# One copy of the head weights, modulation items in four pairs, and eight expert places in a one-core transformer block

## The chip, the cores and the metric

The kernel runs on one core of a Trainium2 chip. The metric is the device time of one execution in microseconds (us), the median of several. A profile of one execution gives its span, from the first to the last instruction, and a trace of every instruction. PE is TensorE, DVE is VectorE, ACT is ScalarE, POOL is GpSimd, SP is SyncE, whose queue issues nearly all loads here.

## The reference

One layer on 256 tokens of width 1024, all in float32:

```python
mod = c_act @ w_ada + b_ada                      # 6 x 1024: shift, scale, gate for both halves
h = rms_norm(x) * (1 + scale1) + shift1
z = h @ w_in                                     # 3 conv inputs, q/kv latents, rope key, 2 gates
merged = sigmoid(zg_conv) * conv_branch + sigmoid(zg_mla) * attention_branch   # 8 heads of 128
x = x + gate1 * (merged @ w_o)
h2 = rms_norm(x) * (1 + scale2) + shift2
x = x + gate2 * moe(h2)                          # 4 groups x 8 experts, top 1 group, top 2 experts
```

Each of the 32 experts has a gate-up matrix (1024 x 512) and a down matrix (256 x 1024).

## The kernel before, in words

Each engine has one instruction stream, written out by hand with semaphores between them. The work goes through five stages.

**Prologue.** Four of the twelve modulation items (`ada_half`, 2 MiB each) and the latent projections run on PE as their weights land.

**Eight heads.** PE's loop over `h` does for each head: the q and k projections, attention output of the head before (`attend`), tile 0 of the next head's five input projections (`conv_tile(h + 1, 0, ...)`, each 8 contraction steps), the v projection (`v_ready`), sums of squares, tiles 1 (`zxc_ready`) and 2, then a wait on `kq_ready` and the scores (`s_ready`), the column sums of one modulation item, tile 3 (`zbg_ready`), tile 4 (`zgm_ready`), and the transposes of the probabilities. In the last head `project_early` puts parts of the output projection in the place of the next head's tiles. A multiplication of 128x128 by 128x256 in float32 is recorded as two instructions.

The other eight modulation items are summed on DVE: `ada_steps` multiplies eight slices of 512 columns with a column of the conditioning vector and adds them up. Steps 0 to 4 stand behind `conv_gated` of the head before; steps 5 to 7 (L1042, L1044) stand ahead of the rotary part of q (L1064, L1065), the reciprocal (L1069) and the normalised keys (L1070, L1071), the last of which gives `kq_ready`. Then come the convolution taps (L1012 to L1016) and the reductions of the scores (L1086, L1088).

The weights of a head (3 MiB: five tiles of 0.5 MiB and the small q, kv matrices) go in one piece into one of the two halves of `wmix`, while the other half is in use. A modulation item goes in one piece (2 MiB) into the region of expert place 3. SP's loop over `c` issues: item `c + 1` after `ada_summed`, weights of head `c + 2` after `v_ready`, and for `c` 1 to 3 expert `c - 1` whole (3 MiB).

**Transition.** The output projection ends; DVE adds it to x (L1120); ACT squares; PE forms the router's logits and sums of squares (`lgt_ready`); DVE copies them (L1126); PE folds them; ACT and DVE do the routing; `select` (L1180 to L1184) gives the first one-hot selection (`sel_ready`). In the meantime PE turns x into rows (`turn_x2`) and opens the four output banks: `open_with_residual` starts tiles 2, 3, 6, 7 with x, `open_empty` starts two banks with nothing.

**Experts.** Tokens of each expert are gathered in windows of 32. A window does on PE: the gate-up product (64 instructions of 128x128), the next window's `gather`, a transpose, `combine` of the window before, `turn_rows`, the down product. Every expert has at least one window; here 35 windows run, and the trace shows experts 2, 3 and 28 with two each. Expert `e` lies in place `e % 7`: four places in `wex`, two in `wmix`, and one split over `act2` and `work`. SP's `next_expert` loads expert `e + 7` into the place of expert `e` as soon as its windows are through: gate-up after `gu_ready`, down after `down_ready`, or both in one piece after `down_ready` in the middle of the list. Half of expert 28's down matrix is loaded ahead into free tiles of `xT`. The loop runs 4 times over 7 places and 4 more experts are written out behind it.

**End.** Two output banks are added to x by DVE and stored by SP; two are copied by ACT (L528) and stored by ACT's queue.

Of the kernel before, what the change touches and what calls it, by code (L numbers as in the profile page):

```python
# [6 lines left out]
I32 = mybir.dt.int32  # L7
# [6 lines left out]
P = 128  # L14
# [48 lines left out]
WO_COLS = KT * 4 * P  # L63
GU_COLS = 2 * KT * FF
DOWN_COLS = (FF // P) * D
EX_SLOTS = 7
OWN = 4
WINDOWS = EXPERTS + SLOTS // WIN
GATE_HEAD = HEADS - 2
FIRST_TILES = 2 * KT * P  # L70
TAIL = EXPERTS - EXPERTS % EX_SLOTS
WORK = 6824
# [3 lines left out]
def block_kernel(nc, xT_d, pos_d, small_d, const_d, ada_d, lat_d, mix_even_d, mix_odd_d, wo_d, ex_d, out_d):  # L76
    with ExitStack() as ctx:
# [8 lines left out]

        wex = sb("wex", [P, OWN, GU_COLS + DOWN_COLS])
        wmix = sb("wmix", [P, GU_COLS + DOWN_COLS + MIX_COLS[0]])
        ring_slot = [wmix[:, 0:GU_COLS + DOWN_COLS], wmix[:, GU_COLS + DOWN_COLS:]]

        ex_place = [wex[:, s, :] for s in range(OWN)] + [ring_slot[1 - s][:, 0:GU_COLS + DOWN_COLS] for s in range(2)]
# [11 lines left out]
        c_rep = sb("c_rep", [P, KT, WIN])  # L103
# [15 lines left out]

        q_lat = piece(3 * T).rearrange("p (k n) -> p k n", k=3)  # L120
# [4 lines left out]
        q_x = piece(T)  # L125
# [5 lines left out]
        v_sb = piece(2 * P).rearrange("p (a b) -> p a b", a=2)  # L131
        rms = piece(2 * T)
        rk_s, rk = rms[:, 0:T], rms[:, T:2 * T]
        scores = piece(P + T)
        probs = piece(P + T)
        pT = piece(P + T)
        zx = piece(T)
        t_gate = piece(T)
        m_gate = piece(T)
        conv_t = piece(T)  # L140
        o_t = zx
        u = piece(T + 2)
        stat = piece(16)
        posi, posf = q_x.bitcast(I32), k_r
# [17 lines left out]
        e_work = piece(2 * 64).rearrange("p (a t n) -> p a t n", a=2, t=TT)  # L162
        s_work = piece(24).rearrange("p (a t) -> p a t", a=12)
        oh = piece(3 * 64).rearrange("p (a t n) -> p a t n", a=3, t=TT)
        slots = piece(64).rearrange("p (t n) -> p t n", t=TT)
        slot_oh = piece(128).rearrange("p (c t n) -> p c t n", c=2, t=TT)
        slot_tok = piece(4).rearrange("p (c t) -> p c t", c=2)
        turn_by = hT[:, 0:KT // 2, :].rearrange("p a n -> p (a n)").rearrange("p (k c) -> p k c", k=KT)
        x2_sq = [hT[:, 4:6, :], hT[:, 6:8, :], comb_both.rearrange("p (k n) -> p k n", k=2), work[:, TT * WIN + 4 * WIN:TT * WIN + 4 * WIN + 2 * T].rearrange("p (k n) -> p k n", k=2)]
        logits_t, sq_sums = hT[:, 4, :], hT[:, 5, :]  # L170
        rs_tok, r_tok = s_work[:, 10, :], s_work[:, 11, :]
        split_tail = piece(GU_COLS // 2 + DOWN_COLS)

        split_head = act2[:, 0:KT, :].rearrange("p a n -> p (a n)")

# [1173 lines left out]
```

## Time and profile before

| | |
|---|---|
| time, median of 3 runs | 501.27 us (500.9 to 501.34) |
| span of the profiled execution | 499.3 us |
| time of the profiled execution by itself | not given; the median run is 2.0 us above the span |
| PE busy | 481.4 us, 96% of the span |
| DVE, ACT, POOL busy | 241.3, 136.6, 152.8 us |
| read from HBM | 160.5 MB, 324 GB/s over the span |
| mean granted clock of PE | 0.992 |

PE is the engine that nearly always works, so a change shows where it alters a wait of PE. The slices of the DMA line say in which stages transfers run without a pause. Of 1 MiB transfers the bytes are 1,048,576.

### The profile page before, as it was taken

Reading aid. Unit: us, or ns where it says so; the run is one execution under the profiler, and the core shown is the slowest. Engines: PE = TensorE matmul, PEld = TensorE weight load, DVE = VectorE, ACT = ScalarE, POOL = GpSimd, SP = SyncE. Lnnn points to the kernel's source line nnn. Section 1 sums busy time; section 2 is a strip of 40 time slices with the busy share of each in tenths; the row PEclk is TensorE's granted clock in tenths of the full one; section 3 lists DMA queues with packets and bytes.
Section 4 is the critical chain, followed back from the end, with each engine's and each line's share of the span. In section 5 each row is a group of like instructions: output and inputs, shape, how many; then the busy total and the mean of one; then the engine's idle time right before and its main releaser. Section 6 shows DMA issues by size and latency. Waiting matters only on the chain.

```text
span 499.3 us, 14059 instructions
## 1 busy us (share of the span) xinstructions
PE 481.4 (96%) x5769; PEld 378.1 (76%) x5770; DVE 241.3 (48%) x647; ACT 136.6 (27%) x243; POOL 152.8 (31%) x195
## 2 busy tenths in 40 slices
PE   8899999999999999999999999999999999888895
PEld 6678888888888888888888877767767766556563
DVE  1433765656565656456651455344344344332343
ACT  4013122323222232313232362232232232221231
POOL 0000010101010101010100018777777777665673
PEclk9999999999999999999999999999999999998998
DMA  8999318295969590907073999899999999999992
GB/s 324 423 424 425 164 53 379 58 433 202 427 258 425 219 407 25 408 8 296 42 291 130 362 411 430 358 394 422 434 437 427 421 441 427 421 423 428 424 403 95
DMA packets 13711, 162.02 MB, mean 324 GB/s; under 512 B 1648, under 2 KB 1904, under 8 KB 3568
## 3 DMA queue, kind: packets, MB, share of 16 engines
q1 hardware_dynamic: 13392, 161.04, 78.1%
q8 instruction: 24, 0.39, 0.3%
q10 hardware_dynamic: 288, 0.52, 0.3%
q14 instruction: 7, 0.06, 0.0%
HBM read 160.51 MB, written 1.05 MB: 324 GB/s over the span
## 4 chain that ended last, share of the span: by engine, by line
PE 83%; DMA 14%; DVE 2%; ACT 0%; issue 0%; ACTq 0%; DVEq 0%
PE ps L536 79%; DMA wex<-in_ex 14%; PE ps L839 1%; PE ps L879 1%; PE ps L840 1%; DVE work L958 0%; ACT xT L528 0%; PE ps L755 0%; PE ps L753 0%; PE ps L754 0%; DVE act L973 0%; DVE act L961 0%; PE ps L739 0%; ACT work L431 0%; DVE work L1223 0%
## 5 line engine op out<-in xcount | busy, mean ns | idle before, releaser
L536 PE MATMUL ps<-act,wmix 128*128 128x256 f32 x864 | 195.0, 381 | 1.7 <-DVE act L973 1.7
L536 PEld LDWEIGHTS ps<-act,wmix 128*128 128x128 f32 x864 | 161.1, 190 | 25.9 <-issue 4.6
L412 POOL TENSOR_SCALAR work<-trig,work 128x256 f32<-128x256 f32 x70 | 64.9, 937 | 57.3 <-issue 48.1
L398 POOL TENSOR_TENSOR work<-work,trig 64x256 f32<-64x256 f32 x8 | 5.8, 719 | 237.0 <-ACT work L466 141.6
L536 PE MATMUL ps<-work 32*128 32x256 f32 (+6 forms) x864 | 72.8, 374 | 0.6 <-DVE work L1223 0.6
L536 PE MATMUL ps<-wex,work 128*32 128x128 f32 (+1 forms) x1824 | 65.6, 295 | 3.7 <-DMA wex<-in_ex 3.7
L536 PEld LDWEIGHTS ps<-wex,work 128*32 128x32 f32 x1824 | 49.8, 110 | 16.8 <-issue 8.4
L536 PEld LDWEIGHTS ps<-work 32*128 32x128 f32 (+3 forms) x864 | 47.6, 168 | 13.3 <-issue 3.3
L524 ACT ACTIVATE work<-ps 128x64 f32<-128x64 f32 x35 | 7.8, 224 | 139.9 <-PE ps L879 139.9
L524 ACT ACT_TABLE_LOAD x35 | 44.9, 1283 | 1.8 <-issue 0.3
L416 POOL TENSOR_TENSOR work<-work,trig 128x512 f32<-128x512 f32 x35 | 44.5, 1271 | 0.0
L536 PE MATMUL ps<-act,work 128*32 128x256 f32 (+1 forms) x704 | 42.9, 362 | 0.9 <-DVE work L1183 0.6
L419 POOL TENSOR_TENSOR work<-work 128x256 f32<-128x256 f32 x35 | 25.5, 727 | 37.3 <-PE ps L536 37.2
L1042 DVE SCALAR_TENSOR_TENSOR wex<-wex,c_rep 128x512 f32<-128x512 f32 x48 | 36.0, 751 | 1.6
L536 PE MATMUL ps<-wmix,work 128*32 128x128 f32 (+2 forms) x704 | 33.3, 304 | 3.3 <-DMA wmix<-in_ex 3.3
L1208 DVE COPY work<-ps 128x128 f32<-128x128 f32 x35 | 10.2, 292 | 54.2 <-PE ps L536 54.2
L536 PEld LDWEIGHTS ps<-wmix,work 128*32 128x32 f32 (+1 forms) x704 | 27.0, 121 | 8.4 <-issue 5.6
L1216 DVE TENSOR_TENSOR work<-ps,mod 128x256 f32<-128x256 f32 x35 | 14.9, 425 | 33.9 <-PE ps L840 33.9
L536 PEld LDWEIGHTS ps<-act,work 128*32 128x32 f32 x704 | 22.4, 111 | 8.3 <-DVE work L1216 0.7
L1211 DVE COPY work<-ps 128x256 f32<-128x256 f32 x35 | 14.9, 425 | 20.6 <-PE ps L536 20.6
L536 PE MATMUL ps<-work,wmix 128*128 128x256 f32 x104 | 23.8, 379 | 0.0
L536 PEld LDWEIGHTS ps<-work,wmix 128*128 128x128 f32 x104 | 19.2, 190 | 2.3
(200 smaller groups left out, 432.2 us busy)
## 6 DMA issues: line engine op xcount, KB each, us to landing
wex<-in_ex SPq DMA_DIRECT2D x10, 3072.0 KB, 22.4
wex<-in_ex SPq DMA_DIRECT2D x10, 2048.0 KB, 24.1
wex<-in_ada SPq DMA_DIRECT2D x8, 2048.0 KB, 7.7
wmix<-in_ex SPq DMA_DIRECT2D x4, 3072.0 KB, 20.9
wmix<-in_mix_odd SPq DMA_DIRECT2D x4, 3008.0 KB, 15.5
wmix<-in_mix_even SPq DMA_DIRECT2D x3, 3200.0 KB, 16.1
wex<-in_ex SPq DMA_DIRECT2D x9, 1024.0 KB, 11.4
wex<-in_ada SPq DMA_DIRECT2D x8, 1024.0 KB, 16.7
```

Source lines behind the costliest of these rows:

```text
L398: nc.gpsimd.tensor_tensor(k_sq[0:ROPE, :], k_sq[0:ROPE, :], k_rope_sq[0:ROPE, :], ALU.add).then_inc(sq_joined, 1)
L412: nc.gpsimd.tensor_scalar(comb_both[:, rows], slot_row[:, rows], lane_now, None, ALU.is_equal).then_inc(comb_half, 1)
L416: nc.gpsimd.tensor_tensor(comb_both, comb_both, weight_row, ALU.mult).then_inc(comb_pair, 1)
L419: nc.gpsimd.tensor_tensor(comb, comb_both[:, 0:T], comb_both[:, T:2 * T], ALU.add).then_inc(comb_ready, 1)
L524: nc.scalar.activation(silu_t, ps[:, 1, 0:2 * WIN], ACT.Silu).then_inc(silu_done, 1)
L536: return nc.tensor.matmul(out, lhsT, rhs, start=start, stop=stop, **kw)
L839: nc.tensor.transpose(ps[:, 0, P:2 * P], rows_sb[:, 0:P], ident)
L840: nc.tensor.transpose(ps[:, 0, 2 * P:3 * P], rows_sb[:, P:T], ident).then_inc(rows_turned, 1)
L1042: link(v.scalar_tensor_tensor(ada_sum, w[:, k, :], c_rep[:, k, 0:1], ada_sum, ALU.mult, ALU.add))
L1208: v.tensor_copy(gu_sb, ps[:, 0, 0:P]).then_inc(gu_copied, 1)
L1211: v.tensor_copy(rows_sb, ps[:, 3, 0:T]).then_inc(rows_copied, 1)
L1216: v.tensor_tensor(xw_v, xw_ps, shift2, ALU.add).then_inc(xw_ready, 1)
```

## The change

- The weights of a head are held once: `conv_w` (five tiles) and `small_w`. SP loads the next head's tiles 0 and 1, tiles 2 and 3, tile 4 and the small matrices as four transfers, each as soon as PE has read the present head's (`zxc_ready`, `zbg_ready`, `zgm_ready`, `v_ready`).
- A modulation item is loaded as four pairs of slices of 0.5 MiB, through two slots (`ada_pair`). `ada_pair_step(j, i)` on DVE waits for pair `i` and does two slices. Pairs 0 and 1 stand where steps 0 to 4 stood, pair 2 where steps 5 to 7 stood, pair 3 behind `kq_ready`, ahead of the taps.
- One region `wex` holds the head weights, the pairs and six expert places in turn; there are eight expert places. Ahead of the loop over `c`, SP issues half the gate-up of expert 5 and all of expert 4; expert `c - 1` for `c` 1 to 4 comes in two pieces; the down matrix of expert 7 goes into `xT` after `residual_in`, and all eight tiles of x are opened into the output banks.
- The output weights come in five transfers into the freed head weights and pairs.
- The memset of `ycomb` and two small copies stand behind `lgt_ready`.
- Experts run in 4 rounds of 8 with nothing behind them. The results are copied to `out_tiles` in place of an addition.

```diff
-EX_SLOTS = 7
+EX_SLOTS = 8
...
+            tiles_load(0, 0, 2, tiles01_landed)
...
+            small_w_load(0)
             sp.dma_start(small[:, SMALL_FIRST:], small_d[:, SMALL_FIRST:]).then_inc(router_landed, 16)
+            pair_load(0, 0)
+            pair_load(0, 1)
+            sp.wait_ge(zxc_ready, 1)
+            tiles_load(1, 0, 2, tiles01_landed)
+            sp.wait_ge(zbg_ready, 1)
+            tiles_load(1, 2, 2, tiles23_landed)
+            sp.wait_ge(zgm_ready, 1)
+            tiles_load(1, 4, 1, tile4_landed)
+            gu_half_load(OWN + 1, OWN + 1, 0)
+            whole_load(OWN, OWN)
             for c in range(HEADS):
+                sp.wait_ge(pair_summed, 4 * c + 1)
+                pair_load(c, 2)
+                sp.wait_ge(pair_summed, 4 * c + 2)
+                pair_load(c, 3)
+                if 1 <= c <= OWN:
+                    gu_load(c - 1, c - 1)
+                sp.wait_ge(v_ready, c + 1)
                 if c + 1 < HEADS:
-                    beside_load(c + 1)
-                if c + 2 < HEADS:
-                    mix_load(c + 2)
...
+                    small_w_load(c + 1)
+                    sp.wait_ge(pair_summed, 4 * c + 3)
+                    pair_load(c + 1, 0)
+                    sp.wait_ge(zxc_ready, c + 2)
...
+                    sp.wait_ge(pair_summed, 4 * c + 4)
+                    pair_load(c + 1, 1)
+                    if 1 <= c <= OWN:
+                        down_load(c - 1, c - 1)
...
+            wo_load(7, 1, wo_w[7], wo7_landed)
+            sp.wait_ge(pair_summed, 4 * HEADS)
+            wo_load(5, 2, wex[:, ADA_AT:ADA_AT + 2 * ADA_PAIR], wo56_landed)
+            head_load(SPLIT, SPLIT)
+            sp.wait_ge(s_ready, HEADS)
+            tail_load(SPLIT, SPLIT)
+            sp.wait_ge(wo_ready, 1)
+            gu_half_load(OWN + 1, OWN + 1, 1)
+            sp.wait_ge(wo_ready, 2)
+            down_load(OWN + 1, OWN + 1)
+            sp.wait_ge(wo_ready, 4)
+            gu_load(LAST, LAST)
             sp.wait_ge(residual_in, 1)
+            down_load(LAST, LAST)
...
-            open_with_residual(7).then_inc(residual_in, 1)
+            open_with_residual(7)
             pe.wait_ge(lg_done, 1)
-            open_empty(2)
+            open_with_residual(4)
+            open_with_residual(5)
             pe.wait_ge(h2r_copied, 4)
-            open_empty(0)
+            open_with_residual(0)
+            open_with_residual(1).then_inc(residual_in, 1)
...
+            def ada_pair_step(j, i):
+                w = ada_pair[i % 2].rearrange("p (k c) -> p k c", k=2)
+                dve.wait_ge(pair_landed[i % 2], 32 * j + 16 * (i // 2) + 16)
+                if i == 0:
+                    dve.wait_ge(c_ready, 2)
                     dve.wait_ge(ada_done, 4 + j)
+                    link(v.tensor_scalar(ada_sum, w[:, 0, :], c_col[:, 0:1], None, ALU.mult))
+                else:
+                    link(v.scalar_tensor_tensor(ada_sum, w[:, 0, :], c_col[:, 2 * i:2 * i + 1], ada_sum, ALU.mult, ALU.add))
+                v.scalar_tensor_tensor(ada_sum, w[:, 1, :], c_col[:, 2 * i + 1:2 * i + 2], ada_sum, ALU.mult, ALU.add).then_inc(pair_summed, 1)
...
                     link(v.tensor_tensor(q_r, q_x, cos_t, ALU.mult))
-                    ada_steps(h, range(5, KT))
+                    ada_pair_step(h, 2)
                     dve.wait_ge(swap_ready, h // 2 + 1)
...
                 v.tensor_tensor(k_r[rope, :], k_rot[rope, :], rk[rope, :], ALU.mult).then_inc(kq_ready, 1)
+                ada_pair_step(h, 3)
                 if h + 1 < HEADS:
                     conv_taps(h + 1)
...
+            dve.wait_ge(lgt_ready, 1)
+            v.memset(ycomb, 0.0).then_inc(y_copied, 1)
             v.tensor_copy(slot_now, co("slot_no"))
             link(v.tensor_copy(lane_now, co("lane_no")))
-            dve.wait_ge(lgt_ready, 1)
             v.tensor_copy(logits_t, ps[:, 5, 0:T]).then_inc(lgt_copied, 1)
```

## Rows read from the trace of the kernel before

**Rows 1.** The page: busy tenths of PE and of the DMA engines in 40 slices

```profile
PE   8899999999999999999999999999999999888895
DMA  8999318295969590907073999899999999999992
```

**Rows 2.** Busy time in stretches: PE, PEld, DVE, ACT, POOL, then clock, DMA share, GB/s

```profile
110.00:135.00 25.00, 25.00 (x131) 21.34 (x130) 15.05 (x32) 7.55 (x17) 1.40 (x2) 1.00 0.76 310
```

**Rows 3.** Timeline of PE among the experts: start, length, line, tiles, [idle before, releaser]

```profile
430.73 1.95 PE L536 MATMUL ps<-wex,work 128*32 128x128 f32 x64 [1.79 <-DMA wex<-in_ex]
...
450.38 3.29 PE L536 MATMUL ps<-wmix,work 128*32 128x128 f32 x64 [1.85 <-DMA wmix<-in_ex]
...
457.83 1.08 PE L536 MATMUL ps<-act,work 128*32 128x128 f32 x32 [0.26 <-DMA work<-in_ex]
...
465.27 1.95 PE L536 MATMUL ps<-wex,work 128*32 128x128 f32 x64 [1.91 <-DMA wex<-in_ex]
...
485.91 2.82 PE L536 MATMUL ps<-wex,work 128*32 128x256 f32 x80
```

**Rows 4.** Timeline of PE, from head 0's tiles to its scores

```profile
49.63 13.98 PE L536 MATMUL ps<-act,wmix 128*128 128x256 f32 x64
63.44 3.62 PE L536 MATMUL ps<-work,wmix 128*128 128x256 f32 x16
...
72.55 7.07 PE L536 MATMUL ps<-act,wmix 128*128 128x256 f32 x32
79.46 2.05 PE L536 MATMUL ps<-work 128*128 128x128 f32 x8
```

**Rows 5.** Transfers: alone at 323.9 (2 MiB), then KB and us to landing

```profile
L283 SPq DMA_DIRECT2D wex<-in_ex x1: 331/331/331, 323.9 to 323.9; - x1
DMA to landing us min/median/max: 7.5/7.5/7.5
...
wex<-in_ada SPq DMA_DIRECT2D x8, 2048.0 KB, 7.7
...
xT<-in_xT SPq DMA_DIRECT2D x1, 1024.0 KB, 5.0
```

**Rows 6.** Timeline of DVE in head 0

```profile
69.28 1.54 DVE L1042 SCALAR_TENSOR_TENSOR wex<-wex,c_rep 128x512 f32<-128x512 f32 x2
...
72.75 0.42 DVE L1064 TENSOR_TENSOR work<-trig,ps 128x256 f32<-128x256 f32 x1 [1.15 <-PE ps L536]
...
75.94 0.42 DVE L1071 TENSOR_TENSOR work<-trig,work 64x256 f32<-64x256 f32 x1
...
81.55 0.29 DVE L1086 CUSTOM_DVE_ANT_0 work<-ps,const 128x128 f32<-128x128 f32 x1 [2.89 <-PE ps L536]
```

**Rows 7.** Clock and PE's busy time in one stretch

```profile
450.80:454.00 3.20, 3.20 (x65) 0.50 1.01 417
```

**Rows 8.** DVE in head 1; DVE and PE in head 7

```profile
98.80 1.75 DVE L1069 RECIPROCAL work<-work 128x256 f32<-128x256 f32 x1 [2.42 <-ACT work L476]
...
256.32 0.42 DVE L1071 TENSOR_TENSOR work<-trig,work 64x256 f32<-64x256 f32 x1
...
261.82 7.17 PE L536 MATMUL ps<-act,wmix 128*128 128x256 f32 x32
```

**Rows 9.** DVE, then PE, in the transition

```profile
274.46 0.48 DVE L1114 MEMSET work<- 128x512 f32 x1
...
281.17 0.17 DVE L1122 COPY work<-const 128x32 f32<-128x32 f32 x1
...
283.35 0.42 DVE L1126 COPY act<-ps 128x256 f32<-128x256 f32 x1 [1.96 <-PE ps L536]
...
289.27 1.54 PE L536 MATMUL ps<-xT,const 128*128 128x256 f32 x6
290.65 0.50 PE L536 MATMUL ps<-work,const 128*128 128x1 f32 x4
291.79 1.07 PE L536 MATMUL ps<-act,work 128*32 128x256 f32 x16 [0.64 <-DVE work L1183]
```

More of the change, by code:

```diff
@@ L118, in piece @@
             return work[0:parts, a:a + cols]
+        v_sb = piece(2 * P).rearrange("p (a b) -> p a b", a=2)
+        scores = probs = piece(P + T)
+        pT = piece(P + T)
+        zx = piece(T)
+        m_gate = piece(T)
+        stat = piece(16)
+        conv_t = piece(T)
+        o_t = zx
+        u = piece(T + 2)
+        c_rep = work[:, 256:256 + KT * WIN].rearrange("p (k n) -> p k n", k=KT)
+        assert work_at[0] <= WORK - 2 * CHUNK_COLS
+        work_at[0] = WORK - 2 * CHUNK_COLS
         q_lat = piece(3 * T).rearrange("p (k n) -> p k n", k=3)
@@ L187, in block_kernel @@
[L187 to L191 removed]
+            if place == SPLIT:
+                half, at = (split_head, split_tail)[k // (KT // 2)], k % (KT // 2)
+                return half[:, 2 * FF * at:2 * FF * (at + 1)]
+            return (ex_place[place] if place < SPLIT else last_gu)[:, 2 * FF * k:2 * FF * (k + 1)]
@@ L358, in _, with tiles_load @@
-            down_load(OWN - 1, OWN - 1)
-            last = EX_SLOTS - 1
-            sp.wait_ge(merged_ready, HEADS)
-            tail_load(last, last)
-            for n in range(2):
-                sp.wait_ge(wo_ready, 2 * n + 2)
-                whole_load(OWN + n, OWN + n)
-            sp.wait_ge(h2r_ready, 2)
-            sp.wait_ge(lg_ready, 1)
-            head_load(last, last)
+            def tiles_load(h, first, count, landed):
+                at = slice(first * CONV_TILE, (first + count) * CONV_TILE)
+                sp.dma_start(conv_w[:, at], (mix_even_d, mix_odd_d)[h % 2][h // 2][:, at]).then_inc(landed, 16)
@@ L552, in ada_half @@
                     pe.wait_ge(ada_copied, n - 1)
-                last = ada_item(wex[:, n, 0:ADA_COLS], ps[:, (0, 5)[n % 2], 0:P], range(half * KT // 2, (half + 1) * KT // 2))
+                last = ada_item(ex_place[n][:, 0:ADA_COLS], ps[:, (0, 5)[n % 2], 0:P], range(half * KT // 2, (half + 1) * KT // 2))
                 if half == 1:
@@ L905, in _ @@
                     next_bound()
-            for e in range(ROUNDS * EX_SLOTS, EXPERTS):
-                with passes() as n:
-                    window(e % EX_SLOTS, ROUNDS + 1, n, e + 2 if e + 2 <= EXPERTS else None, e == TAIL)
-                next_bound()
             at = pe.snap(bound_at, min_val=1, max_val=WINDOWS)
@@ L1109, in _ @@
                     conv_gated(h + 1)
-                    ada_steps(h + 1, range(0, 5))
+                    for i in range(2):
+                        ada_pair_step(h + 1, i)
             merge(HEADS - 1)
-            v.memset(ycomb, 0.0).then_inc(y_copied, 1)
             v.memset(wins[:, 0:1], 0.0)
+            v.memset(table[0:1, EXPERTS + 1:EXPERTS + 2], 0)
             dve.wait_ge(mod_ready, HEADS)
@@ L1323 @@
     ada = np.stack([kcols(w) for w in first] + [kcols(wa[:, n * 512:(n + 1) * 512]) for n in range(4, ADA_ITEMS)])
-    wo = np.stack([tiles(a["w_o"][0][:, n * 512:(n + 1) * 512], 4) for n in range(2)])
+    wo = tiles(a["w_o"][0], 8)
     gate = a["w_exp_gate"][0].reshape(EXPERTS, KT, P, FF)
```

262 lines of the change are left out of this document (128 added, 134 removed).

## The prediction

> **What bounds the kernel now.** I read the slices of the page first [rows 1]: PE is busy nearly throughout, while the transfers pause again and again among the heads and never among the experts. The stretches then say that PE has no idle time at all in a head [rows 2], with the DMA engines at 0.76. So among the heads PE sets the time, and a transfer or a DVE step costs nothing until it makes PE wait. Last I read PE's timeline among the experts [rows 3]. PE waits there for gate-up weights: 1.79, 1.85, 0.26 and 1.91 us in these rows, and once more for 1.44 us in a like row between the first two, 7.25 us in all. The 64 instructions behind the 1.85 us wait take 3.29 us in place of 1.95, and the 16 behind them 1.46 in place of 1.05, at a granted clock of 0.50 [rows 7]: 1.75 us more. So the transfer stream costs about 9.0 us there. Successive landings of experts lie 7.44 us apart (450.38, 457.83, 465.27) for 3 MiB, so 2.48 us per MiB.
>
> **Eight places, among the experts.** The load released at 323.9 by the second window of expert 3 lands 7.5 us later, like a 2 MiB load alone (7.7) [rows 5]. So the queue had run dry there; from then on it never pauses. Before, this load is expert 10. After, with eight places, it is expert 11, and all earlier ones are through, since expert 10 was released 10.6 us sooner (two windows of 5.3 us) and needs 7.4. The stream is then one expert ahead: expert 28's gate-up lands when expert 27's did, at 457.8 and not 465.3. Expert 28's down matrix now comes whole, so from there to expert 31's gate-up are 9 MiB: 457.8 + 22.3 = 480.1. PE began expert 31's gate-up at 485.91 + 1.0 = 486.9 [rows 3] (that row starts with the 16 down instructions). Four windows lie between it and expert 28's first, 486.9 - 465.3 = 21.6 us; after, PE would come to it at 457.9 + 21.6 = 479.5, so the transfer decides at 480.2. Gain 6.7 us. Bounds: at 1% more bandwidth the stream gives 8; 5.7 if the clock falls at expert 28's wait, which I put at 1.6 us (465.3 - 9.0 = 456.3 for PE against 457.9): 1.75 us lost less 0.7 us of slack. I take 6.7.
>
> **Head 0: expert weights ahead of a pair.** SP issues in order. At the end of tile 4, about 63.6 [rows 4], it issues tile 4 of head 1 (0.5 MiB), half of expert 5's gate-up (1 MiB), expert 4 (3 MiB), and only then pair 2 of item 0 (0.5 MiB). The queue is empty before, as tiles 2 and 3 left 3.5 us earlier. A load alone takes 5.0 us for 1 MiB and 7.5 for 2 [rows 5]: 2.5 plus 2.5 per MiB. The pair lands at 63.6 + 2.5 + 5 x 2.48 = 78.5. DVE wants it at 69.28 [rows 6], and DVE is in order: the rotary part, the reciprocal and the keys stand behind it. From the landing: two slices 1.55 us (the row of two is 1.54), then 3.6 us as from 72.75 to the end of 75.94, so `kq_ready` at 83.7. PE wants it at 79.46, when tiles 1 and 2 are through [rows 4]. PE waits 4.2 us. Behind it pair 3 (1.5) and the taps (1.9) delay the score reductions to 87.2; scores end at 85.7, and the transposes come 9.4 us behind the start of the scores, so nothing more is late. Bounds: 0 if the order of the queue did not hold; 5.5 at 2.6 us per MiB and 0.5 us more of start. I take 4.2.
>
> [...]
>
> **The clock behind that wait.** The only fall of the clock with work waiting came behind a 1.85 us wait; waits of 1.79 and 1.91 us drew none [rows 3, 7]. A wait of 4.2 us is twice as long as any of them, so I take a fall, at the price seen: 1.7 us. Bounds: 0 and, if the low level lasts twice as long, 3.4.
>
> **The other heads.** Tiles 2 and 3, tile 4 and pair 2 (2 MiB) are issued from 3.9 us ahead of a head's start to its start, so pair 2 lands some 4 to 5 us into the head. DVE takes it up 5.8 us in (63.44 to 69.28), about 1 us sooner in an odd head. If it is late, the reciprocal still has 2.4 us of waiting ahead of it [rows 8] and one slice fewer (0.77). Cost nothing; cover about 3 us. A head loads at most 8.1 MiB, 20.1 us of its 25.5. Pair 3 puts 1.5 us ahead of the taps, inside the 2.89 us that DVE waits for the scores [rows 6]. Tiles of the next head have 15 us each to land. In head 7 the output weights of tiles 5 and 6 are issued at 256.7 + 1.6 = 258.3 and land at 263.3; PE wants them six steps into 261.82, at 264.4 [rows 8]. Nothing, with 1.1 us of cover; a microsecond late would cost nothing, two would cost one.
>
> **The transition.** The memset is 0.43 to 0.48 us [rows 9], the two copies 0.2 to 0.25, and they now stand between `lgt_ready` and the copy at 283.35, whose end PE waits for: +0.65. Four openings with x replace two empty ones. An opening is 1.54/3, less overlap 0.43. The three ahead end at 290.6; four more end at 292.3, past the 291.79 at which the selection is ready [rows 9]: +0.5. Bounds 0.8 and 1.5 for both. The windows themselves, the four rounds and the copies at the end change nothing that PE or the last store waits for.
>
> **Sum.** -6.7 + 4.2 + 1.7 + 0.65 + 0.5 = +0.35 us on the 499.3 us span. The median of the runs stands 2.0 us above the span; I keep that: 501.27 + 0.35 = 501.6. A difference under 0.2% (1.0 us) is what this measurement can't tell from none.
>
> **Rivals.**
> - *The pair is not late* (0.14). SP's order stands against it; for it only that no 4.5 MiB lie ahead of a small load in this trace among the heads. Then the 4.2 and the 1.7 fall away: -5.5, 495.7 us.
> - *The clock holds* (0.14). The waits of 1.79 and 1.91 us speak for it, their shortness against. -1.35: 499.9 us.
> - *The clock is low for longer, and again at expert 28* (0.12). +0.35 + 1.7 + 1.0: 504.3 us.
> - *Small transfers are too slow* (0.10): every head waits for pair 2. It decides once pair 2 is more than 3 us later than I reckon. Each 0.5 us beyond costs 3.5 us over seven heads, so 505 us and more. Against it: 1 MiB alone lands in 5.0 us [rows 5], on the line of the 2 MiB loads. [...]
> - My forecast has 0.50.
>
> **Chances.** Within the forecast my error is some 1.2 us either way: of its 0.50, 0.06 is faster by over 0.2%, 0.26 within, 0.18 slower. The case of the holding clock splits 0.09 faster, 0.05 within. With the others: faster 0.29, same 0.31, slower 0.40. The likeliest case alone spans 500.0 to 503.5. The range of all reaches down towards the pair in time and up over the longer fall: 497.0 to 504.5.
>
> **What would show it.** In PE's timeline a wait of about 4 us ahead of head 0's scores, released by DVE, with DVE waiting about 9 us for a transfer ahead of its sixth slice; a granted clock of 0.50 behind it. The first window then starts some 7 us later than before. Among the experts waits of at most 3 us in all, at expert 28 and 31 only. If PE does not wait in head 0, the kernel is faster. If waits for pairs or tiles come in every head, or the waits among the experts stay above 5 us, it is slower.

## The result, and the profile after

The changed kernel takes 545.58 us (median of 4 runs, 543.71 to 547.58) beside 501.3 us for the kernel before on the same chip: ratio 1.0879, interval 1.0841 to 1.0916. That is 44 us slower, where 501.6 us was forecast. The profiled execution has a span of 542.0 us against 499.3, so 42.7 us are to be found in it.

The page of the kernel after, the slices and the queues that answer to [rows 1]:

```profile
PE   8899998999999999999999799985998599859995
...
PEclk9999997999999999999999899997999799979998
DMA  8993694989798987455457299999899999999102
...
q1 hardware_dynamic: 21456, 161.04, 75.2%
q8 instruction: 49, 0.80, 0.6%
```

PE's row now has deep notches among the experts, at even distances, where [rows 1] shows 8 and 9, and the clock dips behind each. The bytes of q1 are what the kernel before moved. The queue of instructions, q8, moved 0.80 MB in 49 transfers; on the page of the kernel before that line reads `q8 instruction: 24, 0.39, 0.3%`. One transfer is 16.3 KB. The trace of the kernel before has 13 of these transfers ahead of the experts, 7 in the first round of its loop (290 to 345 us), none in the three rounds from 345 to 469 us, and 4 behind the loop. After, there are 13, then 8 up to 365 us, and 28 more in the rounds behind.

Head 0, the timelines of DVE and of PE (what answers to [rows 4, 6]):

```profile
78.80 0.75 DVE L1092 SCALAR_TENSOR_TENSOR wex<-wex,c_col 128x512 f32<-128x512 f32 x1 [9.19 <-DMA wex<-in_ada]
...
83.53 0.42 DVE L1123 TENSOR_TENSOR work<-trig,work 64x256 f32<-64x256 f32 x1
```

```profile
84.00 3.06 PE L587 MATMUL ps<-work 128*128 128x128 f32 x8 [3.94 <-DVE work L1123]
```

Pair 2 of item 0 is usable at 78.80, where 78.5 was reckoned, and PE waits 3.94 us for the keys. The scores start at 84.00 instead of 79.46; 0.4 of these 4.5 us come from the prologue, 4.1 from the pair.

The clock behind that wait, and the stretches of PE among the experts (busy PE, PEld, DVE, ACT, POOL, then clock, DMA share, GB/s):

```profile
84.00:92.00 8.00, 8.00 (x27) 5.25 (x28) 4.69 (x15) 1.32 (x5) 0.00 (x0) 0.57 0.41 152
335.00:380.00 45.00, 37.11 (x713) 25.70 (x717) 14.71 (x51) 10.55 (x14) 25.18 (x32) 0.92 0.93 383
...
507.00:533.00 26.00, 26.00 (x571) 18.48 (x571) 11.58 (x40) 6.85 (x10) 20.18 (x25) 1.00 0.01 3
```

And PE's timeline among the experts, where [rows 3] had waits for weights:

```profile
308.31 3.64 PE L587 MATMUL ps<-wex,work 128*32 128x128 f32 x64 [3.93 <-issue]
...
362.61 0.51 PE L587 MATMUL ps<-wex,work 128*32 128x128 f32 x9 [2.07 <-issue]
...
372.62 3.64 PE L587 MATMUL ps<-wex,work 128*32 128x128 f32 x64 [5.82 <-issue]
376.03 1.94 PE L587 MATMUL ps<-act,work 128*32 128x256 f32 x16
...
392.39 1.36 PE L587 MATMUL ps<-wex,work 128*32 128x128 f32 x41 [0.19 <-issue]
...
398.47 1.14 PE L587 MATMUL ps<-wex,work 128*32 128x128 f32 x33 [0.16 <-issue]
...
405.12 0.93 PE L587 MATMUL ps<-wex,work 128*32 128x128 f32 x25 [0.74 <-issue]
...
411.54 0.71 PE L587 MATMUL ps<-work 128*32 128x128 f32 x17 [0.51 <-issue]
...
418.97 0.52 PE L587 MATMUL ps<-wex,work 128*32 128x128 f32 x9 [1.52 <-issue]
...
429.36 3.64 PE L587 MATMUL ps<-wex,work 128*32 128x128 f32 x64 [6.20 <-issue]
...
484.83 3.37 PE L587 MATMUL ps<-wex,work 128*32 128x128 f32 x64 [5.96 <-issue]
```

The waits of PE from 270 us on (us in total, times, longest):

```profile
PE ps L587 <- issue: 29.8, 15, 6.2
```

**Where the 42.7 us are.** The first gate-up starts at 308.31 instead of 294.99, 13.3 us later: 8.0 from the heads (the transposes of head 0's probabilities already come 7.9 later, and it stays so), 1.3 from the transition, 4.0 from the wait at the loop's entry. From there to the last down projection the kernel after takes 227.3 us, the one before 197.9: 29.4 more. That is 25.9 us of waits on issue (29.8 less the one at the entry), plus the low clock behind four long ones. Behind the wait at 372.62, 64 matmuls take 3.64 instead of 1.95 us and the next 16 take 1.94 instead of 1.05: 2.6 us. The same stands behind 308.31 and 429.36; behind 484.83 it is 1.4, as the 16 already take 1.04 there: 9.2 for the four. 25.9 + 9.2 less the 9.0 us that the stream cost before is 26.1 of the 29.4. The rest goes with the short waits: the window with the wait of 1.52 us at 418.97 takes 7.24 us instead of 5.31, so 0.4 us more than the wait explains, and there are eleven of them.

### The profile page after: what moved, and what is told of

The parts are those of the page before. It is cut to its first block, busy times and chain, and to the rows that moved or that the text cites. A ratio compares the mean times of both kernels' runs of the same rounds, so it can differ in the third digit from the quotient of the medians.

```text
span 542.0 us, 14151 instructions
## 1 busy us (share of the span) xinstructions
PE 497.5 (92%) x5773; PEld 387.7 (72%) x5774; DVE 238.8 (44%) x648; ACT 136.7 (25%) x244; POOL 152.4 (28%) x195
## 3 DMA queue, kind: packets, MB, share of 16 engines
HBM read 160.51 MB, written 1.05 MB: 298 GB/s over the span
## 4 chain that ended last, share of the span: by engine, by line
PE 82%; DMA 7%; issue 6%; SPq 2%; DVE 2%; ACT 0%; ACTq 0%; DVEq 0%
PE ps L587 77%; DMA wex<-in_ada 7%; PE ps L935 2%; PE ps L896 2%; PE ps L897 1%; SPq L292 1%; SPq L328 0%; DVE work L1121 0%; SPq L339 0%; ACT wex L579 0%; PE ps L813 0%; PE ps L815 0%; PE ps L814 0%; DVE wex L1093 0%; DVE wex L1092 0%
## 5 line engine op out<-in xcount | busy, mean ns | idle before, releaser
L587 PE MATMUL ps<-act,wex 128*128 128x256 f32 x864 | 197.1, 384 | 1.6 <-DVE act L1024 1.6
L587 PEld LDWEIGHTS ps<-act,wex 128*128 128x128 f32 x864 | 162.7, 192 | 26.6 <-issue 4.9
L587 PE MATMUL ps<-wex,work 128*32 128x128 f32 (+2 forms) x2736 | 112.6, 304 | 29.5 <-issue 29.0
L587 PEld LDWEIGHTS ps<-wex,work 128*32 128x32 f32 (+1 forms) x2736 | 87.8, 117 | 51.7 <-issue 40.1
L587 PE MATMUL ps<-act,work 128*32 128x256 f32 (+1 forms) x704 | 46.4, 372 | 0.0
L587 PEld LDWEIGHTS ps<-act,work 128*32 128x32 f32 x704 | 25.5, 114 | 7.3 <-issue 1.4
L1093 DVE SCALAR_TENSOR_TENSOR wex<-wex,c_col 128x512 f32<-128x512 f32 x32 | 24.1, 752 | 1.1
L1266 DVE COPY work<-ps 128x256 f32<-128x256 f32 x35 | 14.9, 425 | 21.9 <-PE ps L587 21.9
L587 PE MATMUL ps<-work,wex 128*128 128x256 f32 x104 | 23.9, 379 | 0.0
L1092 DVE SCALAR_TENSOR_TENSOR wex<-wex,c_col 128x512 f32<-128x512 f32 x24 | 18.0, 749 | 11.1 <-DMA wex<-in_ada 10.6
L587 PEld LDWEIGHTS ps<-work,wex 128*128 128x128 f32 x104 | 19.2, 190 | 2.5
L1121 DVE RECIPROCAL work<-work 128x256 f32<-128x256 f32 x8 | 14.0, 1754 | 11.9 <-ACT work L527 11.7
```

The costliest lines, as they stand in the source:

```text
L587: return nc.tensor.matmul(out, lhsT, rhs, start=start, stop=stop, **kw)
L1092: link(v.scalar_tensor_tensor(ada_sum, w[:, 0, :], c_col[:, 2 * i:2 * i + 1], ada_sum, ALU.mult, ALU.add))
L1093: v.scalar_tensor_tensor(ada_sum, w[:, 1, :], c_col[:, 2 * i + 1:2 * i + 2], ada_sum, ALU.mult, ALU.add).then_inc(pair_summed, 1)
L1121: link(v.reciprocal(rk, rk_s))
L1266: v.tensor_copy(rows_sb, ps[:, 3, 0:T]).then_inc(rows_copied, 1)
```

## The experiments

Each time is a median beside the kernel before in the same comparison (501.1 to 501.8 us). "Waits" are PE's waits among the experts.

### Is it the code? Written out, padded, and two other suspects

`a_unroll`: the kernel after, its four rounds written out as 32 windows.

```
-            with nc.Fori(0, ROUNDS, engines=[pe.engine], head_slot={pe.engine: 0}) as i:
-                for s in range(EX_SLOTS):
+            for e in range(EXPERTS):
```

> The changed kernel with its 32 experts written out on PE, in place of a loop of 4 rounds over 8 places; nothing else differs. Theory A (code loading): a loop body of 8 windows (8 x 230 recorded PE instructions) doesn't stay in PE's instruction memory, is loaded anew in each round, and PE waits for it. Written out, every instruction is loaded once and in order, as the last four windows of the kernel before were: the waits put down to issue fall from 29.8 us to under 5, and the time to 504 to 508 us. Theory B (the eight places or the smaller descriptor scratch slow the experts by themselves): the time stays above 535 us. Theory C (each jump back costs, not the size): as A in time, but the instruction queue would still carry some 0.8 MB; under A it carries about the same 0.8 MB too, so this run does not tell A from C; the padded loop does.

Measured: 532.92 us, ratio 1.0613 (1.0591 to 1.0635). Better than the loop, but far from the 504 to 508 expected. The wait at the entry is gone, and the others are shorter and still there: 17.3 and 3.2 us, with 0.70 MB on q8. So the jump back is only a part of it. Code in a straight line also comes late, while the stream of weights runs.

`b_pad60`: the kernel before with 60 matmuls at the end of the loop body that are never run; only the body is longer.

```
+                with pe.If(pe.snap(bound_at, min_val=0, max_val=WINDOWS) < 1):
+                    for _ in range(60):
+                        mm(ps[:, 0, 0:P], ident, ident, True, True)
```

> The kernel before (loop over 7 places) with 60 matmuls, some 240 instructions or one window's worth, written into the loop body behind a branch that is never taken; they never run. The next bound is also taken as the larger of 1 and the loaded value. Theory A (size of the body): the body is now as long as that of 8 windows, so the three rounds load it anew: instruction traffic rises from 0.39 MB to 0.6 to 0.8 MB, PE waits for issue some 15 to 30 us, and the time is 515 to 540 us. Theory B and C (places, scratch, jumps): nothing of these is changed, so 501 us within 1 us.

Measured: 544.27 us, ratio 1.0841 (1.0819 to 1.0863), above the 515 to 540 expected. All of the loss, in the old kernel, by code that does nothing. PE's timeline and the queue:

```profile
354.20 3.64 PE L536 MATMUL ps<-wex,work 128*32 128x128 f32 x64 [10.94 <-issue]
...
373.21 1.36 PE L536 MATMUL ps<-wex,work 128*32 128x128 f32 x41 [0.33 <-issue]
...
408.90 3.64 PE L536 MATMUL ps<-wex,work 128*32 128x128 f32 x64 [11.37 <-issue]
```

```profile
q8 instruction: 52, 0.85, 0.7%
```

The same pattern as after: a long wait once a round (10.9 to 11.4 us here and 10.8 to 11.4 in `b_pad32` below, in place of 5.8 to 6.2 after), then short ones, 41.6 us in all. Both jump over their unused part too; that this makes the long wait longer is my guess, no run tests it by itself.

`b_scratch`: the kernel before with the kernel after's `dynamic_dma_scratch_size=1024` and its form of the loop bound (all kernels here that start from the one before have that form).

> The kernel before with the descriptor scratch of the changed kernel (1024) and the bound taken as the larger of 1 and the loaded value. Theory A: no change, 501.3 within 1 us. Theory B (scratch or the register operation slows the experts): some of the 44 us appear, above 510 us.

Measured: 501.12 us, ratio 0.9988 (0.9973 to 1.0003). No effect. Ruled out.

`a_unroll_order`: written out, and the expert loads behind the pairs in head 0.

```
-            gu_half_load(OWN + 1, OWN + 1, 0)
-            whole_load(OWN, OWN)
             for c in range(HEADS):
...
                 pair_load(c, 3)
+                if c == 0:
+                    gu_half_load(OWN + 1, OWN + 1, 0)
+                    whole_load(OWN, OWN)
```

> As a_unroll, and the loads of half of expert 5 and of expert 4 stand behind pairs 2 and 3 of item 0 in SP's order. The queue theory of the prediction: head 0's wait ahead of the scores (4 us) and the low clock behind it go, 6 to 8 us less than a_unroll. Rival (the pair is late for another reason, or the low clock has another cause): within 2 us of a_unroll.

Measured: 524.64 us, ratio 1.0431 (1.0396 to 1.0467): 8.3 us less than `a_unroll`. That is the price of the order in SP's queue with the clock behind it; in the trace of after it is 4.1 us of wait and 3.3 of low clock. The waits on issue stay (18.8 us), now at the pace of the code:

```profile
408.48 1.83 PE L588 MATMUL ps<-wex,work 128*32 128x128 f32 x58 [0.48 <-issue]
415.05 1.61 PE L588 MATMUL ps<-wex,work 128*32 128x128 f32 x50 [0.64 <-issue]
421.34 1.39 PE L588 MATMUL ps<-wex,work 128*32 128x128 f32 x42 [0.36 <-issue]
427.49 1.17 PE L588 MATMUL ps<-wex,work 128*32 128x128 f32 x34 [0.22 <-issue]
```

Behind these waits PE goes on at points 6.2 to 6.6 us apart, while PE runs through 256 instructions in 5.7 by my estimate (5.31 us a window of 240).

### Why is the code late, and how long may the body be?

`a_unroll_light`: as `a_unroll_order`, but each load of experts 8 to 31 brings only a quarter of its bytes. It leaves that out of the computation: those experts run partly on old weights.

```
-                    whole_load(s, e + EX_SLOTS)
+                sp.dma_start(part, ex_d[e + EX_SLOTS][:, 0:GU_COLS // 4]).then_inc(gu_landed[s], 16)
...
+                sp.dma_start(place_down(s)[:, 0:DOWN_COLS // 4], ex_d[e + EX_SLOTS][:, GU_COLS:GU_COLS + DOWN_COLS // 4]).then_inc(down_landed[s], 16)
```

> As a_unroll_order, but each load of experts 8 to 31 brings only a quarter of its gate-up and of its down matrix (0.75 MiB in place of 3), so from expert 8 on the products use partly old weights; PE's program is the same. Theory D (instruction blocks are late because they share the DMA engines with a stream that never pauses): the waits for issue in the straight code, 19.5 us in a_unroll_order, fall under 3 us, and the time from 524.6 to 500 to 506. Rival E (the straight code is too long for PE whatever the queues do: blocks load at a fixed pace): the waits and the 524 us stay.

Measured: 491.33 us, ratio 0.979 (0.9769 to 0.9811), below the 500 to 506 expected. Its stretch from 380 to 430 us, and that of `a_unroll_order` below:

```profile
380.00:430.00 50.00, 50.00 (x1086) 35.22 (x1086) 22.45 (x77) 14.29 (x19) 37.93 (x47) 1.00 0.52 152
```

```profile
380.00:430.00 50.00, 46.09 (x908) 32.11 (x912) 18.31 (x63) 10.62 (x15) 32.38 (x40) 0.97 1.00 424
```

The same code, the same 0.70 MB on q8, and not one wait on issue once the DMA engines are busy at 0.52 instead of 1.00. So in this straight code the blocks are late because of the stream of weights. A block's own transfer takes some 1.0 us beside the full stream and 1.1 beside the light one (43 transfers in 0.5% and 0.6% of 16 engines' span), so it is not slower beside the stream; what is late is its start, and whether it queues at the DMA engines or waits for something else these runs don't separate. The run also shows the floor: 35 windows back to back end at 491.3 us.

`a_cut_order` and `b_cut`: gate-up over 6 of its 8 steps, on the kernel after (with the loads behind the pairs) and on the kernel before. Both leave a quarter of gate-up out. By the same count a window then has 208 instructions, eight of them 1,664.

```
-                for k in range(KT):
+                for k in range(6):
```

> The changed kernel with its loop of 4 rounds over 8 places, expert loads behind the pairs as in a_unroll_order, and the gate-up product over 6 of its 8 contraction steps (the other two are left out), so a window has 32 PE instructions less. The body is then shorter (8 x 213 by my count) than that of seven full windows (7 x 245). Theory A (size): no waits for issue, instruction traffic near 0.4 MB as before, and since the transfers now set the end, it is 4 to 6 us faster than b_cut: one expert ahead less the half down matrix, plus the transition. Rival (eight places cost by themselves): waits for issue stay, or it is no faster than b_cut.

> The kernel before with the gate-up product over 6 of its 8 contraction steps; the control of a_cut_order. PE has 0.44 us less per window, but the transfer stream sets the end: 496 to 499 us, with more waits for gate-up weights than the 7 us of before. If PE set the end it would be 486.

Measured: 501.02 us, ratio 0.9976 (0.9959 to 0.9994), and 498.56 us, ratio 0.9933 (0.9911 to 0.9955). In the first q8 fell to 0.34 MB and the waits on issue to 6.5 us, 4.1 of them at the entry. The size of the body is thus borne out, the time is not: `a_cut_order` was to end 4 to 6 us ahead of `b_cut` and ends 2.5 behind, as its wait at the entry was not foreseen. The gain among the experts can still be read: the one on eight places starts its first gate-up 5.5 us later (300.50 against 294.99) and its profiled span ends 1.1 later (499.9 against 498.8), so 4.4 us were made up (3.0 by the medians, since the profiled `b_cut` is its slowest run), in spite of 2.4 us of waits on issue behind the entry. It waits 11.8 us for weights, the one on seven places 17.1.

`b_pad24` and `b_pad32`: the kernel before with 24 and with 32 never-run matmuls in the body.

> The kernel before with 24 matmuls (96 instructions) behind a branch that is never taken, in the loop body; the bound as in b_pad60. By my count the body is then some 1810 instructions, against 1715 of before and 1960 of b_pad60. Theory A says only that there is a limit between the first and the last. If the limit is seven blocks of 256 (1792), some 30 to 43 us are lost here too; if it is nearer to eight, the time is 501 us. [...]

> The kernel before with 32 never-run matmuls in the loop body, about 1,816 of PE's instructions a round against 1,784 with 24 of them and some 1,926 with 60. If only seven blocks of 256 instructions (1,792) stay beside the running one, blocks are fetched again: q8 moves well over 0.39 MB and the time is over 515 us. If eight blocks (2,048) stay, nothing is fetched again: 0.39 MB and 501 to 503 us.

Measured: 502.18 us, ratio 1.0011 (0.9998 to 1.0025), and 543.49 us, ratio 1.0856 (1.0823 to 1.089). The rows of the queue, of 24 and of 32:

```profile
q8 instruction: 24, 0.39, 0.3%
```

```profile
q8 instruction: 51, 0.84, 0.7%
```

Eight matmuls that are never run, 32 instructions, cost 41 us. With 24 of them nothing is fetched again, and the waits on issue are 1.3 us in all. By my count the bodies have 1,784 and 1,816 instructions (seven windows of 240 are some 1,686 with what the loop itself needs, and a matmul is 4: two records on PE and two weight loads). The end of seven blocks of 256, at 1,792, lies between them. The 1,810 of `b_pad24`'s expectation came from 245 instructions a window; the shift by 16 in 256 says 240. The edge itself is shown only to within these eight matmuls. Eight windows of 240 are 1,920.

### The order alone, and the loop's entry alone

`a_order`: the kernel after in its own loop, with only the order of loads of `a_unroll_order`. It moves the loads of experts 5 and 4; the expectation misnames them.

> The kernel after, in its own loop of eight places, with the loads of expert 7's first half and of expert 6 moved behind pairs 2 and 3 of item 0. Theory: the wait of head 0 goes with the low clock behind it, worth 8.3 us in the written-out kernels, and the fetch stalls among the experts stay as long as they were (some 30 us): 536 to 539 us. Rival: the fetch stalls change with the earlier start by several us either way, since they depend on where blocks are asked for while the stream runs: outside 533 to 542.

Measured: 537.99 us, ratio 1.0715 (1.0667 to 1.0763), 7.6 us less than after, with 32.8 us of waits on issue beside 29.8. The scores of head 0 come without a wait:

```profile
79.70 2.06 PE L588 MATMUL ps<-work 128*128 128x128 f32 x8
```

> The kernel after with one thing changed: the loop's head is not set to the start of a block. The 3.9 us wait at the entry goes, as it did in the folded form (5.8 us with the clock behind it); the fetching again each round stays (q8 0.8 MB, over 20 us of waits on issue): 538 to 542 us. If the place of the head also changes how late the blocks come, it is outside that.

Measured: 538.69 us (537.17 to 544.12), ratio 1.0775 (1.0725 to 1.0825), 6.9 us less than after by the medians and 5.2 by the ratios. The wait at the entry is gone, q8 and the other waits (26.8 us) are not:

```profile
304.37 1.96 PE L587 MATMUL ps<-wex,work 128*32 128x128 f32 x64
...
383.73 1.40 PE L587 MATMUL ps<-wex,work 128*32 128x128 f32 x43 [0.20 <-issue]
...
390.00 1.18 PE L587 MATMUL ps<-wex,work 128*32 128x128 f32 x35 [0.34 <-issue]
```

The interrupted groups have 43 and 35 matmuls left instead of 41 and 33, so the body lies only a few instructions elsewhere. By that reading the setting may add a jump in front of the loop, over the filling up to the block's start; no trace shows the jump itself. The stream is not the cause of this wait: in the trace of after the DMA engines are at 0.24 during it, and one block comes on q8. All kernels here that start from the one after and have the setting wait 3.8 to 4.1 us at the entry; those that start from the one before have the same setting and no such wait. Why, was not found.

### Eight places in a body that fits

A window is so long because gate-up is 32 matmuls of four instructions each (64 records and 64 weight loads in the trace). Fewer, wider matmuls into the four quadrants of PSUM, each holding a part of the sum over k, need fewer; what turns the result then also adds the parts. All of this section's kernels do the whole computation. Those on the kernel after also have the loads behind the pairs and the copy of the logits ahead of the fill and the slot copies.

`a_fold`, `b_fold`: gate-up as 8 matmuls of 512 columns, four turning matmuls in place of the transpose; on eight and on seven places.

```
-                for k in range(KT):
-                    for q in range(4):
-                        last = mm(ps[q * WIN:(q + 1) * WIN, 0, 0:P], xw[:, k, :], place_gu(place, k)[:, q * P:(q + 1) * P], k == 0, k == KT - 1)
+                for k in range(KT):
+                    j = k % 4
+                    last = mm(ps[j * WIN:(j + 1) * WIN, 0, :], xw[:, k, :], place_gu(place, k), k < 4, k >= 4)
...
-                nc.tensor.transpose(ps[:, 1, 0:P], gu_sb, ident).then_inc(gu_turned, 1)
+                for q in range(4):
+                    last = mm(ps[:, 1, q * WIN:(q + 1) * WIN], gu_sb[:, q * P:(q + 1) * P], fold_by, True, True)
+                last.then_inc(gu_turned, 1)
```

> The kernel after with the loads in that order, gate-up as 8 matmuls of 512 columns instead of 32 of 128 (each quadrant of PE holds a partial sum over k) and four matmuls that add the quadrants and turn them in place of the transpose, and the copy of the logits ahead of the fill and the slot copies. About 158 of PE's instructions in a window, 1,270 in a round of eight. If the size of the loop body was the cause, no waits on issue among the experts beyond 1 us in all after the loop's entry, q8 at most 0.35 MB, the experts paced by the stream of weights and their PE: 487 to 494 us. If the eighth place or the order of loads costs something of its own, waits on DMA among the experts and over 498 us.

> The kernel before with the same gate-up form, about 1,110 instructions in a round of seven. The stream of weights bounds it as before (its 17 us of waits at weights stay or grow, since PE's windows get shorter): 494 to 500 us. The difference to the folded kernel after is what eight places and the shorter pile-up of transfers bring, 5 to 8 us by the prediction's terms without the waits of head 0.

Measured: 523.67 us, ratio 1.0448 (1.043 to 1.0467), and 516.23 us, ratio 1.0303 (1.0285 to 1.0322). The code part came out as expected (0.33 MB on q8, no wait on issue behind the entry's 3.8 us), the times (487 to 494 and 494 to 500) did not: with no wait at all PE itself takes 6.05 us a window.

`a_fold2`, `b_fold2`: the same with 16 matmuls of 256 columns that go round the quadrants.

```
+                for g in range(2):
+                    for a in range(0, 2 * T, T):
+                        for j in range(4):
+                            last = mm(ps[j * WIN:(j + 1) * WIN, 0, a:a + T], xw[:, 4 * g + j, :], place_gu(place, 4 * g + j)[:, a:a + T], g == 0 and a == 0, g == 1, skip_group_check=True)
```

> As the folded kernel after (523.7 us), but gate-up in 16 matmuls of 256 columns that go round the four quadrants (190 of PE's instructions in a window, 1,520 in a round of eight). There the 8 matmuls of 512 columns took 2.79 us a window against 1.95 in the kernel before and PE's windows 6.05 us, with no wait on DMA, so PE was the bound. Theory: 256-column matmuls overlap across quadrants as those of the down projection do (16 records of 256 columns in 1.05 us), gate-up takes some 2.1 us, windows 5.3 us or less, nothing is fetched again (q8 at most 0.4 MB), and the stream of weights and PE end together: 494 to 500 us, with the 4 us wait at the loop's entry still in it. Rival: eight full-work places cost something besides code: waits over 1 us among the experts, over 504 us.

> The kernel before with the same 16-matmul gate-up, seven places. Waits at weights as before (17 us in all) or more, since the windows aren't longer: 499 to 503 us. If the stream one expert ahead is worth the 6.7 us forecast, it ends 2 to 5 us later than the same form on eight places with its wait at the entry (some 4 us) counted.

Measured: 523.24 us, ratio 1.0434 (1.0418 to 1.045), and 516.95 us, ratio 1.0313 (1.0297 to 1.0328). Nothing changed, and the expectation rested on a misread row: the 2.79 us had been the 16 records of the down projection and gate-up together. PE's timeline of `a_fold2`:

```profile
484.63 1.91 PE L589 MATMUL ps<-wex,work 128*32 128x256 f32 x32
486.35 1.05 PE L589 MATMUL ps<-act,work 128*32 128x256 f32 x16
487.35 1.08 PE L589 MATMUL ps<-work,const 128*128 128x32 f32 x8
```

Gate-up was never slower (1.91 us). It is the four turning matmuls, 1.08 us where the transpose takes 0.33, which over 35 windows make 26 us.

`a_fold2_entry`: `a_fold2` without the head at a block's start.

> The same as the 16-matmul kernel on eight places, but the loop's head is not set to the start of a block of instructions. If the 3.8 to 4.1 us wait at the loop's entry comes from the jump to a fresh block, it goes or shrinks and with it the low clock of the first window, 3 to 5 us less; if the loop then reaches over more blocks than stay, q8 grows and the time goes over 505 us. If the wait is due to code that is late anyway, nothing changes.

Measured: 517.48 us, ratio 1.0322 (1.0307 to 1.0338), 5.8 us less than `a_fold2`, q8 at 0.33 MB: the entry again.

`a_half`, `b_half`: half-folded. Even or odd k and the left or right half make the four quadrants, and two turning matmuls are enough. Gate-up then has 32 records where it had 64 and the turn 4 where it had 1, each with its weight load, so a window has 182 instructions (the expectation says 184) and a round of eight 1,456; neither has the head at a block's start.

```
+                for k in range(KT):
+                    for half in range(2):
+                        j = 2 * (k % 2) + half
+                        last = mm(ps[j * WIN:(j + 1) * WIN, 0, 0:T], xw[:, k, :], place_gu(place, k)[:, half * T:(half + 1) * T], k < 2, k >= KT - 2)
```

> Eight places, all work done: the two expert loads behind the pairs, the logits copy first, the loop's head not set to a block's start, and gate-up as 16 matmuls of 256 columns into four quadrants (even or odd k, left or right half), turned by two matmuls that also add the two sums over k. About 184 of PE's instructions in a window, 1,470 in a round of eight. PE's window is the 5.31 us of before plus some 0.2 for the two turning matmuls in place of one; 295 + 35 x 5.5 + 1.3 is 489 us of PE time alone. If the stream one expert ahead gives its gain at full work: waits at weights under 6 us, no waits on issue, 489 to 496 us, faster than the kernel before. If the stream bounds as in the kernel before: 499 us or more.

> Seven places with the same gate-up form. PE's windows grow by 0.2 us (7 us in all) and its 17 us of waits at weights shrink by about as much: 500 to 504 us. The distance to the same form on eight places is the eighth place's gain with the shorter pile-up, forecast as 6.7 us less 0.7 to 1.7 for the transition: 4 to 9 us.

Measured: 502.25 us, ratio 1.0019 (1.001 to 1.0027), and 504.31 us, ratio 1.0056 (1.0042 to 1.0071). PE's timeline of `a_half`, then the one wait for weights that is left in `b_half` (us in total, times, longest):

```profile
484.89 0.66 PE L589 MATMUL ps<-work,const 128*128 128x64 f32 x4
...
487.81 1.91 PE L589 MATMUL ps<-wex,work 128*32 128x256 f32 x32
489.54 1.05 PE L589 MATMUL ps<-act,work 128*32 128x256 f32 x16
490.52 0.66 PE L589 MATMUL ps<-work,const 128*128 128x64 f32 x4
```

```profile
PE ps L537 <- DMA wex<-in_ex: 1.5, 1, 1.5
```

A window is 5.63 us (484.89 to 490.52), 0.32 more than before and 0.1 more than expected, 11.2 us over 35 windows. The 489 to 496 us expected were missed for that and for a slip: the sum ended with the 35th window's 5.5 us, and 7.8 us of span lie behind that point. `a_half` waits for nothing among the experts. It starts them 0.8 us later than its twin on seven places (295.80 against 294.98) and ends 2.1 us ahead of it by the medians, where 4 to 9 were expected. PE sets the time nearly throughout in both, so this doesn't show what the eighth place is worth at PE's old pace. It takes the changed layout from 44 us behind the kernel before to 1 us behind it, and no version on eight places that was run beats the kernel before with all the work done. A body in which only three of the eight windows are half-folded (1,746 instructions by the same count, 7 us less of PE's time) was not tried.

## Why the prediction was wrong, by its own steps

**The step that failed** is the one in "The transition": "The windows themselves, the four rounds and the copies at the end change nothing that PE or the last store waits for." The body went from seven windows to eight, and with that PE fetches it again in each round: 0.80 MB on q8 in place of 0.39. By my count the edge lies between 1,784 and 1,816 instructions, about seven blocks. `b_pad60` and `b_pad32` make the whole loss in the kernel before with code that never runs, and `b_pad24`, eight matmuls shorter, makes none (ratio 1.0011). `a_unroll_light` shows the second half: in straight code there are 19.5 us of waits on issue beside a stream that holds the DMA engines at 1.00 (`a_unroll_order`), and none beside one at 0.52. The trace of before could have warned: the 7 blocks of the loop's first round are not fetched again in the three rounds behind it (none from 345 to 469 us), so the body was being kept, and its size was there to be counted.

Two things follow from the runs. A body of about seven blocks is not fetched again, though PE jumps back to its start in each round: `b_pad24` moves 0.39 MB on q8 like the kernel before. And without a jump back the blocks come late as well while the weights stream: 20.5 us of waits in `a_unroll`. How PE keeps and asks for its code was not shown beyond that. No rival had this mechanism, and it is outside all of them.

**Eight places among the experts (-6.7).** In the kernel after it can't be seen: its waits for weights are 0 since PE is late for them anyway. Where the code fits, it shows in part: 3.0 to 4.4 us between `b_cut` and `a_cut_order`, with the work cut, and all 7.25 us of waits at weights gone in `a_half`, with PE slower. The direction is shown, the 6.7 at full work and PE's old speed is not. The folded pair, where PE takes 6.05 us a window, shows nothing of it (`a_fold2_entry` 517.48, `b_fold2` 516.95). What there was to gain is seen in `a_unroll_light`: from its first window's turn to its last it takes 180.7 us (299.10 to 479.78), the kernel before 191.8 (297.74 to 489.52), so the stream cost 11.1 us, 2 more than the 9.0 that the prediction listed.

**The pair in head 0 (+4.2).** Right: landed 78.8 for 78.5, a wait that costs 4.1 us, and it goes when only the queue's order is changed (`a_order`). That the pair would not overtake expert 4 was my assumption; in the trace of after expert 4, issued at 64.9 us, lands 12.5 us later, at 77.4, and the pair, issued at 65.5, 13.2 later, at 78.7.

**The clock behind it (+1.7).** The fall came, the size was off: 0.57 over 84 to 92 us, and 3.3 us of delay between the scores and the transposes of head 0's probabilities, about the upper bound given (3.4). With it the wait costs 7.4 us in the trace and 7.6 to 8.3 in the two comparisons. The step took a low stretch of 3.2 us from [rows 7], of a wait half as long.

**The other heads (0).** Right: the delay is 7.9 us at head 0's transposes and 8.0 at the last head's end, so seven heads with small transfers add 0.1.

**The transition (+1.15).** 1.3. A wait of PE for the logits' copy, 0.42 us, stands where reckoned:

```profile
292.47 1.05 PE L587 MATMUL ps<-const,wex 128*128 128x36 f32 x8 [0.42 <-DVE wex L1181]
```

**Not in the sum at all:** the 3.9 us at the loop's entry with the clock behind it, 5.2 to 6.9 us in `a_entry`.

## What to carry to other kernels

Count the instructions of a loop body before adding to it, in blocks of the engine's code, and compare the instruction queue's bytes on the page before and after: a body that stayed cost nothing, eight matmuls more cost 41 us here. The page counts the blocks on the same 16 engines as the data (q8, 0.6% of them after). Written out, they came late beside the stream at 1.00 (20.5 us of waits on issue in `a_unroll`) and never at 0.52, so here the kernel that streamed at full bandwidth paid for its code even without the loop. Where a body must grow, wider instructions buy the room (1,456 instructions for eight windows of `a_half`, by my count, for some 1,920), priced by what must then be added up (0.32 us a window there). And a small load that something in order waits for goes ahead of large ones whose use is far off: 7.6 us between after and `a_order`.

## What the runs showed of the hardware

- The edge is sharp: 32 never-run instructions of PE moved the time from 502.2 to 543.5 us. I had expected the cost of longer code to grow with its length.
- Beside a stream at 424 GB/s PE went on at block boundaries 6.2 to 6.6 us apart, each time behind a wait (`a_unroll_order`); beside one at 152 GB/s it never waited for a block (`a_unroll_light`). The block's own transfer took some 1.0 and 1.1 us.
- The entry into the loop with `head_slot` cost 3.9 us in the kernel after, with the DMA engines at 0.24, and nothing in the one before. This is open.
- Behind each of the long waits among the experts of the kernel after (3.9 us or more) the granted clock fell to 0.50 (0.56 over the stretch behind 484.83), and the next gate-up took 3.4 to 3.64 us in place of 1.95; behind those up to 2.1 us in the kernel after it did not, whereas the kernel before had it fall behind 1.85 us [rows 3, 7] and `a_unroll` to 0.56 behind 2.27 us.
- Turning through PE: two matmuls of 64 columns took 0.66 us and four of 32 columns 1.08 us, though both write 128 columns in all. The transpose that they replace, one record of 128 columns, takes 0.33.
